# A two-block diffusion transformer forward pass: every third weight slab's low half computed on GpSimd from the context's first projection on

## The chip, the cores and the metric

One core of one Trainium2 chip runs one launch. The metric is the device time of that launch in microseconds (us). Times of single instructions are in us or ns as the profile gives them.

## What is computed

The reference runs two small transformer stacks one after the other on 256 latent tokens and 256 context tokens of width 1024, in float32. The first stack has two layers: adaptive norm, SwiGLU feed-forward (width 2816), a mixer (differential attention beside an mLSTM, then gated linear attention), and a second SwiGLU. The second stack has two layers: multi-head latent attention (MLA) and a 4096-wide squared-ReLU MLP, then neighbourhood attention (NA) and another such MLP, with layer norms after each. Every layer's shifts, scales and gates come from a modulation vector, `silu(c) @ ada_w + ada_b`. The second stack's context stream starts from its own input (`ctx_2`), so its first projections do not depend on the latents that leave the first stack.

```
h = x * (1 + sc1) + sh1;  y, yc = mixer(h, hc)
x = layer_norm(alpha * x + g1 * y)
x = layer_norm(alpha * x + g2 * (relu((x*(1+sc2)+sh2) @ w1)**2 @ w2))
```

## The kernel before, in words

**Split products.** All weights are streamed in 620 slabs of 128x1024 float32 in the order in which they are used (`PLACE` maps a slab's name to its number). Each float32 product is made of three products of TensorE's reduced-precision float32 format (fp32r): ScalarE copies the slab into fp32r (`split_high`, L1614), VectorE subtracts that from the slab to get the low half (`split_low`, L2026), and TensorE computes high x high, high x low and low x high (L2612, L2613, L2614). The activations are split the same way (`h_high`/`h_low`, L2121 and L2113; `hidden_high`/`hidden_low`, L1717 and L2219). A slab feeds 24 matmuls of 256 columns, or half as many of 512.

**One written order.** `order()` yields the steps of the whole pass, and `schedule()` turns each `done` step of a slab s (TensorE has finished with it) into a fetch of slab s+8, `split_high` of s+5 and `split_low` of s+4. Every engine's program walks through this one list and takes the steps that are its own, in order; waits between engines are semaphore counts (`wait_ge`, `mark`). There are 8 raw buffers, 8 low buffers and 6 high buffers: `split_high(s)` waits for the load and for TensorE to have finished slab s-6.

**What each engine does in the order.** ScalarE: `split_high`, activations, squares, high halves. VectorE: `split_low`, the residual additions (L2229), the product after SiLU or ReLU (`mult`/`relu`, L2207 and L2214, one input in PSUM), `hidden_low`, the norms, softmax maxima, and the modulation: for the blocks n = 24 to 239 of the modulation a dot product with the condition vector (`ada`, L2040, shown as CUSTOM_DVE_ANT_0 with two SBUF inputs), one per stream. GpSimd (`pool_program`): the chains of additions for the norms (`add_up`, L1494, one 128x256 addition per feature tile), the scaling of the residual (`plain`, L1557), the rotary products (L1515, L1518), and the loads of the even modulation blocks (`load_ada`, L1472). SyncE issues all other loads, the odd modulation blocks among them. A load of block n waits until VectorE has finished block n-6, since there are six buffers.

**The second stack** interleaves streams: the context's MLA projections and attention run between pieces of the latents' last SwiGLU (`beside_ffn11`), the latents' MLA between pieces of the context's MLP (`beside_mla`), then the latents' MLP with the modulation of the last layer, blocks 204 to 239 (`beside_mlp0`, `ada_pieces`), then NA (`na_steps`) and the last MLP. A layer norm (`layer_norm_groups`) needs two chains of seven GpSimd additions, one for the mean (`add_mean`, then TensorE's `mean_sum`, L2698) and one for the squares (`centre`, then `sum_of_squares`, L2665). For the last two layer norms (`ln10`, `ln11`) VectorE adds the first chain and GpSimd only the squares (`near_centre`); TensorE then reads both sums (`near_sums`, L2684 and L2688).

```
if step[0] == "done" and s + RAWS < N_SLABS:
    yield "fetch", s + RAWS
ahead = HIGHS - 1 if step[0] == "done" else 0
while n_high <= min(s + ahead, N_SLABS - 1):
    yield "split_high", n_high
    n_high += 1
while n_low <= min(s + max(ahead - 1, 0), N_SLABS - 1):
    yield "split_low", n_low
    n_low += 1
```

Of the kernel before, what the change touches and what calls it, by code (L numbers as in the profile page):

```python
# [8 lines left out]
F32 = mybir.dt.float32  # L9
# [20 lines left out]
RAWS, HIGHS = 8, 6  # L30
# [1048 lines left out]
PLACE = places()  # L1079


def schedule():

    n_high = n_low = HIGHS - 1
    for step in order():
        if step[0] not in ("done", "ready"):
            yield step
            continue
        s = PLACE[step[1]]
# [9 lines that stand above are left out]
# [5 lines left out]
class Signal:  # L1104
# [8 lines left out]
    "gla_gate", "ctx2", "na_bv", *(f"rpb{i}" for i in range(4)), "stored",  # L1113
    "gemm", "summed", "swapped", "gates_turned", "scored", "turned", "weighed", "squares_added", "g_spread",
    "spread", "decay_in", "keys_turned", "inner_scored", "state_in", "inner_out", "chunk_in", "chunk_out",
    "split_high", "split_low", "cond_silu", "ada_dot", "ada_block", "mods", "scales", "gates", "squared", "added", "mean", "root", "rstd", "rstd_spread",
    "scaled", "h_high", "h_low", "silu", "relu", "relu_squared", "hidden_raw", "hidden_high", "hidden_low", "x_new",
    "x_final", "x_scaled", "plain", "centred", "near_added", "less_added", "last_added", "ln_scaled", "ln_out", "fm_act", "fm_dve", "tm_act", "tm_dve",
    "gate_act", "gate_dve", "fcol", "floor_act", "lambda_dve", "lambda_act", "rope_sin", "rope_cos", "roped",
# [358 lines left out]
def pool_program(m, pool):  # L1478
# [29 lines left out]
    def near_centre(tag, k, p):  # L1508
        if k < DT - 1:
            square(tag, k, p)  # L1510

    def rope(which, j, bank):
        x, tmp = rope_tile(m, which, j), rope_temp(m, which, j)
        pool.wait_ge("swapped", (which, j))
        do.tensor_tensor(x, x, m.C("cos"), ALU.mult).then_inc(*pool.mark("rope_cos", (which, j)))  # L1515
        pool.wait_ge("rope_sin", (which, j))
        pool.wait_ge("rope_cos", (which, j))
        do.tensor_tensor(x, x, tmp, ALU.add).then_inc(*pool.mark("roped", (which, j)))  # L1518
# [34 lines left out]
    def plain(tag, k, p):  # L1553
        if p not in PLAIN[tag][1]:
# [1 line left out]
        pool.wait_ge("plain", (tag, k, p))  # L1556
        do.tensor_scalar(m.x[:, k, COLS[p]], m.x[:, k, COLS[p]], ALPHA, None, ALU.mult).then_inc(*pool.mark("x_scaled", (tag, k, p)))  # L1557

    work = {"ada": ada, "square": square, "add_mean": add_mean, "centre": centre, "near_centre": near_centre,
            "rope": rope, "da_normalise": da_normalise, "ml_normalise": ml_normalise, "even_norm": even_norm,  # L1560
            "gla_decay3": gla_decay3, "gla_factors": gla_factors, "plain": plain}
    for name, *args in schedule():
# [456 lines left out]
def vector_program(m, dve):  # L2019
    do = dve.do  # L2020
    last_low = [None]

    def split_low(s):
        i = s % RAWS
        dve.wait_ge("split_high", s)
        do.tensor_tensor(m.low[i][:, :], m.raw[i][:, :], m.high[s % HIGHS][:, :].bitcast(F32), ALU.subtract).then_inc(  # L2026
            *dve.mark("split_low", s))
# [571 lines left out]
def tensor_program(m, pe):  # L2599
# [21 lines left out]
    def h_product(bank, tag, s, p):  # L2621

        free(bank)
        pe.wait_ge("split_low", s)
        return products(m.bank[bank][:, 0:T if p == BOTH else NC_TOK], [
            (("h_low", (tag, k, p) if p in H_PARTS.get(tag, (0, 1)) else (tag, k)), *columns_of(s, k), *m.h_term(k, p)) for k in range(DT)])

# [89 lines left out]
    def down(f, c, k, p, bank, at):  # L2717
        n, cols = SIZES[f][c], m.hidden_cols(f, p)
        if at == 0:
            free(bank)  # L2720
        for t in range(at, min(at + 8, n)):
            b = k * n + t
            s, h = PLACE[down_slab(f, c, b)], chunk_at(f, c) + t
            i = h % n_hidden(f)
            pe.wait_ge("split_low", s)
            pe.wait_ge("hidden_low", (f, h))
            last = products(m.bank[bank][:, 0:T if p == BOTH else NC_TOK], [
                (None, *columns_of(s, b % 8), m.hidden[f][i][:, cols], m.hidden_low[f][i][:, cols])],
                start=t == 0, stop=t == n - 1)
            keys = [("x", f, c, k, p), ("down", f, c)] if t == n - 1 else []  # L2730
            if b % 8 == 7:
                keys.append(s)
            if keys:
                last.then_inc(*pe.mark("gemm", *keys))
        read[bank] = "x_new", ("x", f, c, k, p)
# [6 lines left out]
    def out(name, k, half, p, bank):  # L2742
        halves, tag = OUT_HALVES.get(name), H_OF[name]
        keys = [("x", name, k, half, p), *(("out", name, k, half, part) for part in STREAMS_OF[p])]
        if halves:
            s, first = PLACE[SLAB0[name] + 4 * half + k // 2], halves[half]
            free(bank)
            pe.wait_ge("split_low", s)
            terms = [(("h_low", (tag, first + i)), *columns_of(s, k % 2 * 4 + i), *m.h_term(first + i, out_part(name, first + i, p))) for i in range(4)]
            last = products(m.bank[bank][:, 0:T if p == BOTH else NC_TOK], terms)  # L2750
            keys += [s] if k % 2 else []
        else:
            s = PLACE[SLAB0[name] + k]
            last = h_product(bank, tag, s, p)
            keys.append(s)
# [2 lines left out]

    def tm(name, g, half, i, s, banks):
        stage, (_, first, k_slabs, _), s = stage_of(name), TM[name], PLACE[s]  # L2760
        pe.wait_ge("split_low", s)
        for t in range(2):
            tt, bank = 2 * half + t, banks[t]
            if bank is None:
# [257 lines left out]

    def uq(p, i, t, bank):
        s, tag = PLACE[uq_slab(p, i)], of(p, "mla_c")
        pe.wait_ge("split_low", s)
        free(bank)
        products(m.bank[bank][:, 0:NC_TOK], [(("h_low", (tag, k)), *columns_of(s, 2 * k + t), *m.h_term(k, p)) for k in range(4)]
                 ).then_inc(*pe.mark("gemm", ("uq", p, i, t), *([s] if t else [])))
# [1 line left out]

    def uk(p, i, t, bank):
        s, tag = PLACE[SLAB0[of(p, f"mla_uk{i}")]], of(p, "mla_c")
        pe.wait_ge("split_low", s)
        free(bank)
        products(m.bank[bank][:, 0:NC_TOK], [(("h_low", (tag, 4 + k)), *columns_of(s, 4 * k + t), *m.h_term(4 + k, p)) for k in range(2)]
                 ).then_inc(*pe.mark("gemm", ("uk", p, i, t), *([s] if t == 3 else [])))
# [91 lines left out]
```

## Time and profile before

| | |
|---|---|
| median of 3 runs | 2941.49 us (2940.67 to 2943.84) |
| the profiled execution, its own time | 2941.7 us |
| its span, first to last instruction | 2939.9 us |
| busy: PE, VectorE (DVE), ScalarE (ACT), GpSimd (POOL) | 96%, 68%, 43%, 12% |
| mean granted TensorE clock | 0.98 of full |
| slabs whose low half VectorE makes | 620, of which slab 264 is the context's first MLA projection |

PE is TensorE's matmul row and PEld its weight load. A row of a timeline gives the start and the duration in us, the engine and line, the operation, and in brackets the idle time of the engine before it with what ended it. 1704 us is where the low half of slab 264 is computed, so that the stretch from 1704 us to the end at 2940 us is the one in which the change acts.

### The profile page before, as it was taken

The numbers are of one execution on the slowest core, as the hardware profiler recorded it, in microseconds if no ns is written. First come the engines' busy times: TensorE is split into PE (matmuls) and PEld (weight loads), VectorE is DVE, ScalarE is ACT, GpSimd is POOL, SyncE is SP. The second block draws the span as 40 slices with busy tenths as digits, with TensorE's granted clock in tenths as the row PEclk, the third lists the DMA queues.
The fourth block names the chain that finished last, engine by engine and source line by source line (L and its number), as shares of the span: only waits on it lengthen the run. The fifth ranks groups of instructions, "written<-read, shape, count | busy, mean of one in ns | idle before, by whom it ended". The sixth has DMA issues, their size and how long they took to land.

```text
span 2939.9 us, 43428 instructions
## 1 busy us (share of the span) xinstructions
PE 2831.9 (96%) x17424; PEld 2475.1 (84%) x17424; DVE 2010.9 (68%) x3382; ACT 1276.7 (43%) x2094; POOL 340.2 (12%) x380
## 2 busy tenths in 40 slices
PE   7999999988999999999999989999999999999998
PEld 6888897545888889888897889999979999887898
DVE  7789955645687646788655775666656688767764
ACT  4222234443422234222245565556455554645653
POOL 0000010321100001000011110022102210300100
PEclk8999999988999999999999999999999999999999
DMA  6666522101355544555432234455525579553453
GB/s 245 222 224 230 198 86 91 51 29 44 130 206 208 201 143 149 203 202 207 156 106 82 70 132 150 149 180 173 165 78 174 186 279 330 192 155 101 136 187 115
DMA packets 141191, 467.59 MB, mean 159 GB/s; under 512 B 27024, under 2 KB 29200, under 8 KB 140480
## 3 DMA queue, kind: packets, MB, share of 16 engines
q1 hardware_dynamic: 125440, 408.20, 40.9%
q0 software_dynamic: 15552, 56.63, 5.5%
q8 instruction: 138, 2.26, 0.3%
q14 instruction: 61, 0.50, 0.1%
HBM read 463.73 MB, written 1.05 MB: 158 GB/s over the span
## 4 chain that ended last, share of the span: by engine, by line
PE 80%; DVE 11%; ACT 5%; issue 2%; DMA 2%; POOL 1%; SPq 0%; ACTq 0%; DVEq 0%; POOLq 0%
PE bank L2612 24%; PE bank L2614 24%; PE bank L2613 24%; DVE sb_split_low L2026 3%; DVE sb_h_low L2113 1%; PE bank L2902 1%; DMA sb_raw<-weights 1%; PE bank L2883 1%; PE bank L3049 1%; DMA sb_ada_mlp<-ada 1%; PE bank L2843 1%; DVE sb_temp L2040 1%; DVE sb_temp L2107 1%; POOL sb_temp L1494 1%; ACT sb_temp L1931 1%
## 5 line engine op out<-in xcount | busy, mean ns | idle before, releaser
L2612 PE MATMUL bank<-sb_h_high,sb_split_high 128*128 128x256 f32 (+1 forms) x3392 | 1101.8, 325 | 35.2 <-DVE sb_h_low L2121 11.8
L2613 PE MATMUL bank<-sb_h_low,sb_split_high 128*128 128x256 f32 (+1 forms) x3392 | 1085.1, 320 | 0.0
L2614 PE MATMUL bank<-sb_h_high,sb_split_low 128*128 128x256 f32 (+1 forms) x3392 | 1084.6, 320 | 0.0
L1614 ACT ACTIVATE sb_split_high<-sb_raw 128x1024 fp32r<-128x1024 f32 x620 | 646.5, 1051 | 307.8 <-PE bank L2614 288.6
L2026 DVE TENSOR_TENSOR sb_split_low<-sb_raw,sb_split_high 128x1024 fp32r<-128x1024 f32 x620 | 758.7, 1232 | 18.7 <-ACT sb_split_high L1614 18.6
L2612 PEld LDWEIGHTS bank<-sb_h_high,sb_split_high 128*128 128x128 f32 x3392 | 653.1, 193 | 95.2 <-issue 12.5
L2613 PEld LDWEIGHTS bank<-sb_h_low,sb_split_high 128*128 128x128 f32 x3392 | 653.8, 193 | 43.4
L2614 PEld LDWEIGHTS bank<-sb_h_high,sb_split_low 128*128 128x128 f32 x3392 | 653.2, 193 | 43.5
L2040 DVE CUSTOM_DVE_ANT_0 sb_temp<-sb_ada_ffn,sb_cond_ffn 128x1024 bf16<-128x1024 f32 x364 | 429.4, 1218 | 22.8 <-DMA sb_ada_ffn<-ada 22.2
L2612 PE MATMUL bank<-sb_hidden_high_ffn,sb_split_high 128*128 128x512 f32 (+1 forms) x830 | 280.4, 338 | 0.0
L2614 PE MATMUL bank<-sb_hidden_high_ffn,sb_split_low 128*128 128x512 f32 (+1 forms) x830 | 279.2, 336 | 0.0
L2613 PE MATMUL bank<-sb_hidden_low_ffn,sb_split_high 128*128 128x512 f32 (+1 forms) x830 | 279.1, 336 | 0.0
L2229 DVE SCALAR_TENSOR_TENSOR sb_x_res<-bank,sb_gates,sb_x_res 128x256 f32<-128x256 f32 x288 | 132.1, 478 | 172.1 <-PE bank L2614 171.8
L1717 ACT ACTIVATE sb_hidden_high_ffn<-sb_temp 128x512 fp32r<-128x512 f32 (+1 forms) x94 | 52.1, 554 | 339.9 <-DVE sb_temp L2207 339.9
L1704 ACT ACTIVATE sb_temp<-bank 128x256 f32<-128x256 f32 (+1 forms) x158 | 72.8, 461 | 290.3 <-PE bank L2614 290.1
L2207 DVE TENSOR_TENSOR sb_temp<-sb_temp,bank 128x512 f32<-128x512 f32 (+1 forms) x94 | 55.5, 590 | 201.8 <-PE bank L2614 201.3
L2613 PEld LDWEIGHTS bank<-sb_hidden_low_ffn,sb_split_high 128*128 128x128 f32 x830 | 156.3, 188 | 18.6
L2612 PEld LDWEIGHTS bank<-sb_hidden_high_ffn,sb_split_high 128*128 128x128 f32 x830 | 156.2, 188 | 18.6
L2614 PEld LDWEIGHTS bank<-sb_hidden_high_ffn,sb_split_low 128*128 128x128 f32 x830 | 156.2, 188 | 18.5
L2612 PE MATMUL bank<-sb_hidden_high_mlp,sb_split_high 128*128 128x256 f32 x512 | 144.8, 283 | 3.9 <-DVE sb_hidden_low_mlp L2219 3.9
L1472 POOL DMA_DIRECT2D sb_ada_ffn<-ada x90 | 47.8, 532 | 844.6 <-DVE sb_ada_col L2040 844.6
L2614 PE MATMUL bank<-sb_hidden_high_mlp,sb_split_low 128*128 128x256 f32 x512 | 144.0, 281 | 0.0
(329 smaller groups left out, 3487.7 us busy)
## 6 DMA issues: line engine op xcount, KB each, us to landing
sb_raw<-weights SPq DMA_DIRECT2D x620, 512.0 KB, 3.4
sb_ada_ffn<-ada SPq DMA_DIRECT2D x114, 512.0 KB, 4.6
sb_ada_ffn<-ada POOLq DMA_DIRECT2D x90, 512.0 KB, 3.6
sb_ada_mlp<-ada POOLq DMA_DIRECT2D x18, 512.0 KB, 5.5
sb_ada_mlp<-ada SPq DMA_DIRECT2D x18, 512.0 KB, 5.9
sb_cond_ffn<-cond SPq DMA_DIRECT2D x3, 1024.0 KB, 5.4
sb_na_raw<-na_rpb SPq DMA_DIRECT2D x32, 96.0 KB, 6.6
sb_x_res<-tokens SPq DMA_DIRECT2D x4, 512.0 KB, 7.1
```

Of the source, the lines that this page charges most:

```text
L1472: lane.do.dma_start(m.ada[f][i][:, :], m.w["ada"][n, :, :]).then_inc(*lane.mark(ada_signal(n), n, step=16))
L1494: do.tensor_tensor(acc, other if k == 1 else acc, new, ALU.add).then_inc(*pool.mark("added", (kind, tag, k, p)))
L1614: do.activation(m.high[s % HIGHS][:, :], m.raw[s % RAWS][:, :], identity).then_inc(*act.mark("split_high", s))
L1704: do.activation(m.hidden_temp(f, h, p), src, func).then_inc(*act.mark(name, (f, h, p)))
L1717: do.activation(m.hidden[f][i][:, m.hidden_cols(f, p)], m.hidden_temp(f, h, p), identity).then_inc(*act.mark("hidden_high", (f, h, p)))
L2026: do.tensor_tensor(m.low[i][:, :], m.raw[i][:, :], m.high[s % HIGHS][:, :].bitcast(F32), ALU.subtract).then_inc(*dve.mark("split_low", s))
L2040: do.tensor_tensor_reduce(out=m.junk(s), in0=m.ada[f][i][:, :], in1=m.cond[f][:, s, :], scale=1.0, scalar=0.0, op0=ALU.mult, op1=ALU.add, ...
L2207: do.tensor_tensor(temp, temp, src, ALU.mult).then_inc(*dve.mark("hidden_raw", (f, h, p)))
L2229: do.scalar_tensor_tensor(x, m.bank[bank][:, bank_cols(p, s)], m.gates_of(stage)[:, k, s:s + 1], x, ALU.mult, ALU.add).then_inc(*dve.mark( ...
L2612: do.matmul(out, ah, bh, start=start and j == 0, stop=False)
L2613: do.matmul(out, ah, bl, start=False, stop=False)
L2614: last = do.matmul(out, al, bh, start=False, stop=stop and j == len(terms) - 1)
```

## The change

A function names, for a slab, the signal under which its low half is announced: `split_low_pool` for slabs from the context's first projection on (number 264) whose number is divisible by three, `split_low` for all others. VectorE skips the former. `pool_program` gets a `split_low` step that does the same subtraction for them, at the same place of the written order and after the same wait for `split_high`. Each place of `tensor_program` that waits for a slab's low half waits for the named signal.

```diff
+def low_signal(s):
+
+    return "split_low_pool" if s >= PLACE[SLAB0["cmla_down"]] and s % 3 == 0 else "split_low"
...
-    "split_high", "split_low", "cond_silu", "ada_dot", "ada_block", "mods", "scales", "gates", "squared", "added", "mean", "root", "rstd", "rstd_spread",
+    "split_high", "split_low", "split_low_pool", "cond_silu", "ada_dot", "ada_block", "mods", "scales", "gates", "squared", "added", "mean", "root", "rstd", "rstd_spread",
...
+    def split_low(s):
+        if low_signal(s) != "split_low_pool":
+            return
+        i = s % RAWS
+        pool.wait_ge("split_high", s)
+        do.tensor_tensor(m.low[i][:, :], m.raw[i][:, :], m.high[s % HIGHS][:, :].bitcast(F32), ALU.subtract).then_inc(
+            *pool.mark("split_low_pool", s))
...
-    work = {"ada": ada, "square": square, "add_mean": add_mean, "centre": centre, "near_centre": near_centre,
+    work = {"split_low": split_low, "ada": ada, "square": square, "add_mean": add_mean, "centre": centre, "near_centre": near_centre,
...
     def split_low(s):
+        if low_signal(s) != "split_low":
+            return
         i = s % RAWS
         dve.wait_ge("split_high", s)
...
-        pe.wait_ge("split_low", s)
+        pe.wait_ge(low_signal(s), s)
```

The last replacement stands in `h_product`, `down`, `out`, `tm`, `uq` and `uk` alike.

## Rows read from the trace of the kernel before

**Rows 1.** Windows: length, then PE, PEld, DVE, ACT, POOL busy, clock, DMA share, GB/s.

```profile
1704.00:2940.00 1236.00, 1188.97 (x9241) 1128.15 (x9240) 844.55 (x1384) 666.07 (x1141) 156.74 (x158) 0.99 0.52 170
2375.00:2510.00 135.00, 131.13 (x1085) 130.32 (x1084) 123.73 (x197) 61.73 (x93) 7.92 (x15) 0.99 0.85 305
```

**Rows 2.** Waits of the weight loads, 1704 to 2940 us: total, times, longest.

```profile
PEld bank L2612 <- DVE sb_h_low L2121: 10.8, 11, 2.0
...
PEld bank L2612 <- DVE sb_ctx_temp L2214: 5.8, 4, 2.2
...
PEld bank L2612 <- DVE sb_hidden_low_mlp L2219: 4.7, 4, 2.5
...
PEld bank L2612 <- DVE sb_split_low L2026: 3.6, 2, 1.9
```

**Rows 3.** Windows of line L2026 alone (the low halves on VectorE).

```profile
2375.00:2510.00 135.00, 55.77 (x46) 0.99 0.85 305
```

**Rows 4.** Line views of GpSimd's two-input operations: min/median/max ns, first and last start, forms.

```profile
L1494 POOL TENSOR_TENSOR sb_temp<-sb_temp,sb_square x94: 721/740/1774, 393.0 to 2917.3; 128x256 f32<-128x256 f32 x94
L1544 POOL TENSOR_TENSOR sb_odd_big<-sb_odd_big x4: 1263/1266/1288, 1553.9 to 1657.9; 128x512 f32<-128x512 f32 x4
```

**Rows 5.** Timeline: VectorE and GpSimd at 1709 us, then both at 2329 us.

```profile
1710.00 0.96 DVE L2121 TENSOR_TENSOR sb_h_low<-sb_temp,sb_h_high 128x256 fp32r<-128x256 f32 x1
...
1709.48 1.20 POOL L1494 TENSOR_TENSOR sb_temp<-sb_temp,sb_square 128x256 f32<-128x256 f32 x1 [0.22 <-ACT sb_square L1628]
...
2329.36 1.22 DVE L2026 TENSOR_TENSOR sb_split_low<-sb_raw,sb_split_high 128x1024 fp32r<-128x1024 f32 x1
...
2329.52 1.64 POOL L1494 TENSOR_TENSOR sb_temp<-sb_temp,sb_x_res 128x256 f32<-128x256 f32 x1 [1.20 <-DVE sb_x_res L2229]
```

**Rows 6.** Timeline of VectorE in the latents' MLP: one up piece, and the next one's start.

```profile
2399.58 0.41 DVE L2214 TENSOR_TENSOR sb_temp<-sb_temp,bank 128x256 f32<-128x256 f32 x1
2399.91 1.21 DVE L2040 CUSTOM_DVE_ANT_0 sb_temp<-sb_ada_mlp,sb_cond_mlp 128x1024 bf16<-128x1024 f32 x1
...
2401.05 0.41 DVE L2219 TENSOR_TENSOR sb_hidden_low_mlp<-sb_temp,sb_hidden_high_mlp 128x256 fp32r<-128x256 f32 x1
2401.39 1.21 DVE L2026 TENSOR_TENSOR sb_split_low<-sb_raw,sb_split_high 128x1024 fp32r<-128x1024 f32 x1
2402.53 0.41 DVE L2214 TENSOR_TENSOR sb_temp<-sb_temp,bank 128x256 f32<-128x256 f32 x1
```

**Rows 7.** VectorE's longest waits from 2370 to 2510 us, and the loads' times to landing.

```profile
DVE sb_temp L2040 <- DMA sb_ada_mlp<-ada: 7.6, 8, 1.4
DVE sb_hidden_low_mlp L2219 <- ACT sb_hidden_high_mlp L1717: 1.9, 4, 0.5
...
DMA to landing us min/median/max: 4.1/5.8/7.3
```

**Rows 8.** Timeline: loads of blocks 226 (GpSimd) and 227 (SyncE), their dots, and ScalarE's slab 486.

```profile
2440.64 0.53 POOL L1472 DMA_DIRECT2D sb_ada_mlp<-ada  x1 [7.53 <-DVE sb_ada_col L2040]
...
2456.51 0.43 SPq L1472 DMA_DIRECT2D sb_ada_mlp<-ada  x1
...
2460.41 1.22 DVE L2040 CUSTOM_DVE_ANT_0 sb_temp<-sb_ada_mlp,sb_cond_mlp 128x1024 bf16<-128x1024 f32 x1
...
2463.42 1.21 DVE L2040 CUSTOM_DVE_ANT_0 sb_temp<-sb_ada_mlp,sb_cond_mlp 128x1024 bf16<-128x1024 f32 x1
...
2452.57 1.04 ACT L1614 ACTIVATE sb_split_high<-sb_raw 128x1024 fp32r<-128x1024 f32 x1
```

**Rows 9.** Timeline at two layer norms: GpSimd's last additions and the matmul that needs them.

```profile
1913.63 1.64 POOL L1494 TENSOR_TENSOR sb_temp<-sb_temp,sb_x_res 128x256 f32<-128x256 f32 x1 [0.35 <-DVE sb_x_res L2229]
...
1915.74 0.59 PE L2698 MATMUL bank<-sb_temp,sb_const 128*128 128x256 f32 x2
...
2723.98 5.47 POOL L1494 TENSOR_TENSOR sb_temp<-sb_temp,sb_square 128x256 f32<-128x256 f32 x5 [0.59 <-ACT sb_square L1628]
...
2729.79 0.61 PE L2684 MATMUL bank<-sb_const,sb_rstd 128*128 128x1 f32 x4 [1.63 <-DVE sb_rstd L2157]
```

More of the change, by code:

```diff
@@ L2724, in down @@
             i = h % n_hidden(f)
-            pe.wait_ge("split_low", s)
+            pe.wait_ge(low_signal(s), s)
             pe.wait_ge("hidden_low", (f, h))
@@ L2747, in out @@
             free(bank)
-            pe.wait_ge("split_low", s)
+            pe.wait_ge(low_signal(s), s)
             terms = [(("h_low", (tag, first + i)), *columns_of(s, k % 2 * 4 + i), *m.h_term(first + i, out_part(name, first + i, p))) for i in range(4)]
@@ L2760, in tm @@
         stage, (_, first, k_slabs, _), s = stage_of(name), TM[name], PLACE[s]
-        pe.wait_ge("split_low", s)
+        pe.wait_ge(low_signal(s), s)
         for t in range(2):
@@ L3024, in uq @@
         s, tag = PLACE[uq_slab(p, i)], of(p, "mla_c")
-        pe.wait_ge("split_low", s)
+        pe.wait_ge(low_signal(s), s)
         free(bank)
@@ L3032, in uk @@
         s, tag = PLACE[SLAB0[of(p, f"mla_uk{i}")]], of(p, "mla_c")
-        pe.wait_ge("split_low", s)
+        pe.wait_ge(low_signal(s), s)
         free(bank)
```

## The prediction, made before the changed kernel ran

> **What bounds the kernel now.** I read the windows first, then the waits, then the timelines of the places they point to. In the stretch where the change acts the weight loads fill 1128 of 1236 us at a clock of 0.99, and VectorE 845 us [rows 1]. TensorE sets the time, then, and VectorE can give back only what TensorE waits for it. That is little: the four largest such waits are 10.8, 5.8, 4.7 and 3.6 us, 25 us in all [rows 2]. Only 3.6 us name the low half itself. The reader is to see that 119 subtractions leave VectorE (slabs 264 to 618, every third), at 1.14 us of queue each (from 2401.39 to 2402.53) [rows 6] 136 us of its work, and that a gain has at most 25 us, and most likely a third of that, to come from.
>
> One window is different. From 2375 to 2510 us, the latents' MLP with the last modulation blocks, VectorE is busy 123.7 of 135 us [rows 1], and its idle time is waiting for modulation loads (7.6 us) and for ScalarE (1.9 us) [rows 7], hardly for TensorE. In an up piece its instructions stand back to back: product, dot, hidden low half, slab low half, 2.95 us from one product to the next (2399.58 to 2402.53) [rows 6]. TensorE needs less: 135 us less the 4.7 it waits [rows 1, 2], over 1085 matmuls, is 0.12 us a matmul, and 24 of them, a slab, are 2.88 us. There VectorE is as much the bound as TensorE, and those 4.7 us are TensorE waiting for hidden low halves [rows 2].
>
> **The price of the moved instruction.** No row shows a 128x1024 operation on GpSimd. Alone, 256 columns take 740 ns (the median) and 512 take 1263 [rows 4]. The line through both gives 740 + 3 x 523 = 2.31 us. The ends are VectorE's 1.22 us [rows 5], were the format or size to favour it, and 4 x 0.74 = 2.96 us. I take 2.31, because both sizes lie on one line with a small fixed part.
>
> **What it does to VectorE.** The timelines show the two engines stopping each other. A VectorE subtraction of 256 columns takes 0.96 us at 1710.00, behind GpSimd's addition, where the usual one takes 0.43; and GpSimd's addition of 0.74 us takes 1.64 when it begins 0.16 us into a VectorE subtraction of 1.22 [rows 4, 5]. In the latter case 1.22 - 0.16 = 1.06 us of waiting plus 0.74 is 1.80, so GpSimd stood still nearly all the time and then ran. I take it that one waits for the other, full length, when both read two SBUF tensors. Products with an input in PSUM go on. The Trainium skill (SBUF — State Buffer, section "SBUF: two separate sides") calls the shared port pair "an exclusive lock, not a bandwidth split", held for the whole instruction; it speaks against this change, and the rows agree within their 0.2 us. Under that rule the sum is the one below, and under plain sharing it would be the faster rival's.
>
> **Term A, 2375 to 2510 us.** 46 low halves fall in it [rows 3], so 15 move. Each frees 1.14 us of VectorE. Its operation on GpSimd, 2.31 us, starts when VectorE's running subtraction ends; the product beneath it goes on (0.33 us, from 2399.58 to 2399.91), then the dot waits for the rest, 1.98 us [rows 6]. Net 1.98 - 1.14 = +0.84 us, times 15 = +12.6 us of VectorE. Of that its 7.6 us of waiting for loads are absorbed [rows 7], since SyncE issues the odd blocks at TensorE's pace and a later VectorE finds them landed: +5.0.
>
> The even blocks' loads sit in GpSimd's queue and are moved too, past its new waits. Today GpSimd runs ahead: block 226 is issued at 2440.6 for a dot at 2460.4, while SyncE's block 227 is issued at 2456.5 for a dot at 2463.4 [rows 8]. Behind the subtraction of slab 486, whose high half ScalarE ends at 2453.6, block 226 cannot go before 2453.6 + 2.3 = 2455.9; with the median 5.8 us to landing it is there at 2461.7, 1.3 us late, and with 7.3 us 2.8 late [rows 7, 8]. Going through all 18 even blocks in this way, with each one's own time to landing, I find three or four late by 1 to 3 us and the rest early by 0.5 to 10: +3. Nothing is lost if VectorE lags anyway; if GpSimd's operation itself waits 1.1 us each time, some eight are late and it is +8. **Sum of A: +8** (0 to +20).
>
> **Term B, the norms' chains.** GpSimd now puts a 2.3 us subtraction inside chains of additions that TensorE waits for. In the context's first layer norm the last addition ends at 1915.27 and the matmul that needs it starts at 1915.74 [rows 9]: under 0.5 us to spare, and slab 321's subtraction stands between two of the additions. The chain idles some 0.35 us ahead of each pair and saves a wait or two for VectorE, so +1.2. The latents' first norm has the same pattern (slab 414): +1.4. The square chain of the latents' second norm (slab 513) has about 1.3 us to spare: +1.3. In the NA norm the chain of five additions ends at 2729.45, 0.34 us ahead of the first matmul of the sums [rows 9], slab 558's subtraction stands in it, and no other work covers it: +2.0. In the others the additions come 2.88 us apart or the subtraction falls outside. **Sum of B: +6** (0 to +14).
>
> **Term C, the attention stretches.** VectorE works there in short chains (maximum, reciprocal, scaling, which may wait behind GpSimd) with a subtraction of its own less per moved slab. One against the other: +1 (-2 to +5).
>
> **Term D, what VectorE gives back.** Outside A and B its waits of 10.8, 5.8 and 3.6 us are 17 events [rows 2]; a third of them, about 5 or 6, have a moved subtraction ahead, worth at most 1.14 us each: 6.5, less what is blocked elsewhere: **-5** (-10 to 0).
>
> At no cost, because others cover them: the later low halves themselves. They are made four slabs ahead, 4 x 2.88 = 11.5 us of TensorE, against at most 2.3 + 1.2 us on GpSimd. The 104 moved subtractions outside A fall mostly where VectorE has a third of its time free; if that cover went, each would cost A's 0.84 us.
>
> **Sum.** +8 + 6 + 1 - 5 = +10 us. The profiled execution's own time is 2941.7, so 2951.7 us; it lies 0.2 us above the median, which gives **2951.5 us**.
>
> **The rivals.**
>
> *No change.* TensorE is the bound and the written order has slabs and banks enough: blocks of 2 us on VectorE vanish in its free third. For it: nowhere outside A does VectorE reach 90% for long, and the additions may regroup. Against it: A has no free time at all. It would give A +3, B +3, C 0, D -5: 2942.
>
> *Faster.* The end on the other side: VectorE's queue in A. If GpSimd's subtraction blocked VectorE by less than the 1.14 us it frees, A's step would fall from 2.95 us on average by 0.2, under TensorE's 2.88, and the 4.7 us of waiting for hidden halves would go; the same freedom gives D its full 6.5. 2941.5 - 11 = 2930. It decides at a block of 1.14 us per moved slab. Against it: the 0.96 us subtraction at 1710 [rows 5].
>
> *The loads decide.* GpSimd's loop in A, high half, subtraction (2.3, or 3.5 when it waits), load (5.8), dot, becomes the pace, so that eight even blocks come late and each lateness reaches TensorE: A +16, the rest as forecast: 2960. For it: SyncE's loads already land just as VectorE asks [rows 7]. Against it: GpSimd's queue passes a moved slab only every third slab.
>
> That the change does nothing of what it says I exclude: the test on the slab's number is the same for maker, skipper and reader.
>
> **How the numbers follow.** Forecast 0.44, no change 0.27, faster 0.15, the loads 0.14. A measurement of this kernel tells about 0.2% (5.9 us) from none, so the bounds are 2935.6 and 2947.4. The forecast's own range, from its terms, is 2944 to 2962; I count its lower edge with the slower side. Hence faster 0.15, same 0.28, slower 0.57. The range reaches down into the no-change case and nearly to the faster one, 2936, and up past the loads, 2966.
>
> **What would show it.** The new subtractions on GpSimd: 119 at 2.3 us alone, up to 3.5 when VectorE runs; VectorE's own busy time in the last 1236 us down by less than 145, with dots and subtractions of over 2 us among them (a blocked instruction shows as a long one). In A: the waits of TensorE for hidden low halves up from 4.7 to about 12 us, GpSimd's waits for the dots (block n-6) gone and even loads landing within some 3 us of their dots. In the NA norm: the first matmul of the sums 2 us later against the last product before it. I am wrong if dots and low halves on VectorE keep their 1.22 us, if the waits in A do not grow, or if the norm chains end as early as now.

## The result, and the profile after

The changed kernel takes 2967.49 us (median of 4 runs, 2963.61 to 2971.95), the kernel before 2942.17 us beside it: ratio 1.0084, 95% interval 1.0071 to 1.0098, which is 24.7 us more (0.84% of 2942.17; 20.9 to 28.8). The prediction said 2951.5, between 2936 and 2966. The direction is right, the size is not, and the time lies above the range. The profiled execution took 2966.69 us (span 2964.6).

In the new files the lines have moved by up to 15: the subtraction is L2041 on VectorE and the new one L1522 on GpSimd, the dot L2055, the low halves L2136 and L2234, the first product L2627. First the page of the changed kernel, busy times and the two groups of low halves, then GpSimd's group by line (minimum, median and longest, in ns):

```profile
PE 2841.2 (96%) x17424; PEld 2480.6 (84%) x17424; DVE 1982.2 (67%) x3263; ACT 1276.7 (43%) x2094; POOL 643.9 (22%) x499
...
L2041 DVE TENSOR_TENSOR sb_split_low<-sb_raw,sb_split_high 128x1024 fp32r<-128x1024 f32 x501 | 651.1, 1305 | 22.1 <-ACT sb_split_high L1627 22.1
L1522 POOL TENSOR_TENSOR sb_split_low<-sb_raw,sb_split_high 128x1024 fp32r<-128x1024 f32 x119 | 319.2, 2683 | 645.8 <-ACT sb_split_high L1627 641.7
```

```profile
L1522 POOL TENSOR_TENSOR sb_split_low<-sb_raw,sb_split_high x119: 2339/2682/3489, 1704.3 to 2932.2; 128x1024 fp32r<-128x1024 f32 x119
```

GpSimd got its 119 subtractions: 2.34 us when nothing holds them up, 2.68 in the median, 3.49 at worst. VectorE lost 119 instructions, which should have taken 136 us off its 2010.9 us; it lost 29. The rest came back inside its other instructions, whose work has not changed: a slab's low half, for one, took 1232 ns in the mean before and takes 1305 now. The timelines below show them standing still.

The windows, and VectorE's and the weight loads' waits, of the latents' MLP (2375 to 2510 us before, the same work now from 2382 to 2533):

```profile
core 0: us, PE busy (x) PEld busy (x) DVE busy (x) ACT busy (x) POOL busy (x), PEclk, DMA share, GB/s
2382.00:2533.00 151.00, 135.93 (x1089) 134.06 (x1088) 133.59 (x182) 62.51 (x93) 53.55 (x34) 0.97 0.80 284
```

```profile
engine line waited for: us in total, times, longest us
DVE sb_temp L2055 <- DMA sb_ada_mlp<-ada: 12.1, 7, 2.8
...
PEld bank L2627 <- DVE sb_hidden_low_mlp L2234: 9.1, 5, 3.5
PEld bank L2627 <- issue: 7.8, 5, 4.1
```

Against [rows 1, 2, 7]: the stretch is 151 us in place of 135. VectorE is busy 133.6 in place of 123.7 although 15 or 16 instructions of 1.22 us have gone; its waits for modulation loads are 12.1 us in place of 7.6; TensorE's waits for hidden low halves 9.1 in place of 4.7.

The timelines of GpSimd, VectorE and TensorE in 2466 to 2485 us show both at work:

```profile
2468.23 2.82 POOL L1522 TENSOR_TENSOR sb_split_low<-sb_raw,sb_split_high 128x1024 fp32r<-128x1024 f32 x1 [7.79 <-ACT sb_split_high L1627]
2471.00 0.58 POOL L1477 DMA_DIRECT2D sb_ada_mlp<-ada  x1
2477.25 2.40 POOL L1522 TENSOR_TENSOR sb_split_low<-sb_raw,sb_split_high 128x1024 fp32r<-128x1024 f32 x1 [5.67 <-ACT sb_split_high L1627]
2479.61 0.57 POOL L1477 DMA_DIRECT2D sb_ada_mlp<-ada  x1
2480.20 2.74 POOL L1522 TENSOR_TENSOR sb_split_low<-sb_raw,sb_split_high 128x1024 fp32r<-128x1024 f32 x1
```

```profile
2468.70 0.41 DVE L2229 TENSOR_TENSOR sb_temp<-sb_temp,bank 128x256 f32<-128x256 f32 x1
2469.03 3.10 DVE L2055 CUSTOM_DVE_ANT_0 sb_temp<-sb_ada_mlp,sb_cond_mlp 128x1024 bf16<-128x1024 f32 x1
...
2478.61 2.13 DVE L2055 CUSTOM_DVE_ANT_0 sb_temp<-sb_ada_mlp,sb_cond_mlp 128x1024 bf16<-128x1024 f32 x1 [2.85 <-DMA sb_ada_mlp<-ada]
2480.67 0.08 DVE L2055 DVE_READ_ACCUMULATOR2_ANT sb_ada_col<- 128x1 f32 x1
2480.67 2.56 DVE L2234 TENSOR_TENSOR sb_hidden_low_mlp<-sb_temp,sb_hidden_high_mlp 128x256 fp32r<-128x256 f32 x1
```

```profile
2484.51 0.36 PE L2627 MATMUL bank<-sb_hidden_high_mlp,sb_split_high 128*128 128x256 f32 x1 [3.90 <-DVE sb_split_low L2041]
```

GpSimd's subtraction runs from 2468.23 to 2471.05. The product, with one input in PSUM, begins 0.47 us into it and takes its usual 0.41. The dot, with two inputs in SBUF, takes 3.10 in place of 1.22: it ends 1.08 us after the subtraction, its own length, less the overlap that the records have. Then comes the second effect. GpSimd issues block 226's load (2471.00) only behind that subtraction; in the kernel before this load went out 19.8 us ahead of its dot [rows 8]. VectorE now idles 2.85 us for it. Third, the next subtraction, which starts at 2480.20 while a dot is still running, holds up the hidden low half behind that dot: 2.56 us in place of 0.41. Behind it in VectorE's queue stands the low half of a slab (2483.15, 1.21 us), and for that the matmul at 2484.51 had waited 3.90 us.

TensorE's clock comes on top of the waits. The matmuls at 2484.70 and 2484.82 are 0.12 us apart; soon after that wait of 3.90 us they come every 0.21 us, because the granted clock has fallen to 0.50, the lower of its two levels (1.2 GHz in place of 2.4):

```profile
2485.50:2488.00 2.50, 2.50 (x14) 2.50 (x14) 2.47 (x7) 0.00 (x0) 0.00 (x0) 0.50 0.71 280
```

Over the whole stretch the mean granted clock is 0.97, and 0.99 before. By estimate that costs up to 151 x 0.03 - 135 x 0.01 = 3.2 us of what the stretch loses; up to, because TensorE isn't busy all the time. The prediction had no term for it.

Where the 25 us lie. The table compares the start of the same weight load in two traces, by stretches of the kernel before (us). A trace has some 2 us of its own variation: ahead of 1700 us the kernels do not differ, and in 2375-2510 e2 and e6 show +2.1 each and move nothing there.

| kernel | to 1700 | 1700-1800 | 1800-1960 | 1960-2120 | 2120-2375 | 2375-2510 | 2510-2710 | to the end | sum |
|---|---|---|---|---|---|---|---|---|---|
| changed | -1.2 | +3.2 | +3.0 | +2.3 | -0.1 | +15.6 | -1.7 | +3.4 | +24.7 |
| e1, MLP only | +0.1 | +0.4 | 0.0 | 0.0 | -1.1 | +19.5 | -1.2 | -0.7 | +17.0 |
| e2, all but MLP | +1.0 | +3.3 | +3.1 | +2.2 | -0.3 | +2.1 | -2.0 | +2.1 | +11.4 |
| e3, waits only | +2.8 | 0.0 | 0.0 | 0.0 | -0.2 | +1.4 | +0.6 | +0.2 | +4.9 |
| e4, even loads early | +3.4 | +3.3 | +3.0 | +4.5 | -0.3 | +10.4 | -2.2 | +2.1 | +24.3 |
| e11, all loads early | -2.3 | +3.3 | +3.1 | +4.5 | -0.2 | +4.6 | -2.3 | +2.8 | +13.4 |
| e5, first five | +3.4 | +4.3 | 0.0 | 0.0 | -0.4 | -1.6 | -2.0 | +0.1 | +3.9 |
| e6, spared places | +3.0 | -0.2 | 0.0 | +2.3 | +0.5 | +2.1 | -1.9 | -0.3 | +5.5 |
| e7, no read | +0.8 | -4.4 | -1.0 | -1.5 | -4.7 | -3.9 | -2.8 | -0.9 | -18.4 |
| e9, no read, 8 pieces | +0.8 | -4.4 | -1.0 | -1.5 | -4.6 | -2.6 | -4.4 | -0.8 | -18.4 |
| e12, no read, 32 pieces | +2.7 | -2.4 | -1.0 | -1.5 | -4.1 | -2.8 | -5.3 | -0.2 | -14.6 |
| e8, odd loads early | +0.6 | +0.4 | +0.1 | 0.0 | -1.1 | -5.6 | 0.0 | +0.1 | -5.4 |
| e10, e8 and five moves | +2.4 | -2.7 | +0.1 | -1.5 | -2.1 | -5.6 | -1.6 | -0.7 | -11.5 |

### The profile page after: what moved, and what is told of

It reads as the page before. It is cut to its first block, busy times and chain, and to the rows that moved or that the text cites. A ratio compares the mean times of both kernels' runs of the same rounds, so it can differ in the third digit from the quotient of the medians.

```text
span 2964.6 us, 43436 instructions
## 1 busy us (share of the span) xinstructions
PE 2841.2 (96%) x17424; PEld 2480.6 (84%) x17424; DVE 1982.2 (67%) x3263; ACT 1276.7 (43%) x2094; POOL 643.9 (22%) x499
## 4 chain that ended last, share of the span: by engine, by line
PE 77%; DVE 11%; ACT 5%; issue 2%; DMA 2%; POOL 1%; SPq 0%; ACTq 0%; POOLq 0%; DVEq 0%
PE bank L2627 23%; PE bank L2629 23%; PE bank L2628 23%; DVE sb_split_low L2041 3%; DMA sb_ada_mlp<-ada 1%; ACT sb_split_high L1627 1%; DVE sb_h_low L2128 1%; PE bank L2917 1%; DVE sb_temp L2055 1%; DMA sb_raw<-weights 1%; POOL sb_temp L1499 1%; PE bank L2898 1%; DVE sb_h_low L2136 1%; PE bank L3064 1%; PE bank L2858 1%
## 5 line engine op out<-in xcount | busy, mean ns | idle before, releaser
L2627 PE MATMUL bank<-sb_h_high,sb_split_high 128*128 128x256 f32 (+1 forms) x3392 | 1102.5, 325 | 40.9 <-DVE sb_h_low L2136 17.4
L2627 PEld LDWEIGHTS bank<-sb_h_high,sb_split_high 128*128 128x128 f32 x3392 | 653.0, 192 | 102.4 <-DVE sb_h_low L2136 18.1
L2041 DVE TENSOR_TENSOR sb_split_low<-sb_raw,sb_split_high 128x1024 fp32r<-128x1024 f32 x501 | 651.1, 1305 | 22.1 <-ACT sb_split_high L1627 22.1
L1522 POOL TENSOR_TENSOR sb_split_low<-sb_raw,sb_split_high 128x1024 fp32r<-128x1024 f32 x119 | 319.2, 2683 | 645.8 <-ACT sb_split_high L1627 641.7
L2055 DVE CUSTOM_DVE_ANT_0 sb_temp<-sb_ada_ffn,sb_cond_ffn 128x1024 bf16<-128x1024 f32 x364 | 429.6, 1220 | 23.1 <-DMA sb_ada_ffn<-ada 14.4
L2627 PE MATMUL bank<-sb_hidden_high_ffn,sb_split_high 128*128 128x512 f32 (+1 forms) x830 | 280.7, 338 | 2.0 <-DVE sb_x_res L2244 2.0
L2627 PEld LDWEIGHTS bank<-sb_hidden_high_ffn,sb_split_high 128*128 128x128 f32 x830 | 156.3, 188 | 21.3 <-DVE sb_x_res L2244 2.8
L2629 PEld LDWEIGHTS bank<-sb_hidden_high_ffn,sb_split_low 128*128 128x128 f32 x830 | 156.3, 188 | 18.4
L2627 PE MATMUL bank<-sb_hidden_high_mlp,sb_split_high 128*128 128x256 f32 x512 | 146.4, 286 | 12.0 <-DVE sb_hidden_low_mlp L2234 8.0
```

The lines of the kernel that those rows point to most:

```text
L2055: do.tensor_tensor_reduce(out=m.junk(s), in0=m.ada[f][i][:, :], in1=m.cond[f][:, s, :], scale=1.0, scalar=0.0, op0=ALU.mult, op1=ALU.add, ...
L2627: do.matmul(out, ah, bh, start=start and j == 0, stop=False)
L2629: last = do.matmul(out, al, bh, start=False, stop=stop and j == len(terms) - 1)
```

## The experiments

The theory after the result: GpSimd's subtraction shuts VectorE's two-input work out for its whole length, which costs where TensorE already hangs on VectorE, and lets the modulation loads slip. The rivals: the longer and more often waiting queue of GpSimd does it without any blocking; or every moved slab costs its share. In the results, "less" and "more" are the ratio times the 2944 us of the kernel before; in brackets stands the 95% interval.

### e1 and e2: the change by place

```diff
-    return "split_low_pool" if s >= PLACE[SLAB0["cmla_down"]] and s % 3 == 0 else "split_low"
+    return "split_low_pool" if 459 <= s <= 504 and s % 3 == 0 else "split_low"
```

e2 moves the others, from 264 on, and leaves 459 to 504.

> Only the slabs 459 to 504 divisible by three go to GpSimd (16 of the 119), those of the latents' MLP in which VectorE has no free time; all others stay on VectorE. Theory (that stretch costs +15.6 us of the 24.7 us between the two traces, because VectorE is the bound there): +13 to +17 us over the kernel before. Rival (the cost is spread evenly, 0.21 us per moved slab): +3 us. Second rival (the lag of 7 us that the changed kernel brings into the stretch is what tips it): +5 to +10 us.

> The other 103 slabs go to GpSimd, 459 to 504 stay on VectorE. Theory: +7 to +10 us over the kernel before. Even spread: +22 us. If the stretches outside were harmless (no change in themselves): 0.

e1: 2958.85 us, ratio 1.0048 (1.0031 to 1.0065), 14.1 us more, as expected. e2: 2954.53 us, ratio 1.0035 (1.0022 to 1.0048), 10.3 us more, just over the 7 to 10 expected. Together 24.4 of the 24.7 us: the two parts add up, and 16 of the 119 moved slabs, those of the latents' MLP, carry more than half. That e1's stretch shows +19.5 us in its trace, more than the changed kernel's +15.6, is in part the clock: its mean is 0.94 there. e2 also shows that the rest is no +2 us, as terms B, C and D had it together, but 10.

### e3: the wait without the subtraction

The kernel before; GpSimd waits for the high halves of the 16 slabs 459 to 504 at the places where the changed kernel subtracts, and does nothing.

```diff
+    def split_low(s):
+        if 459 <= s <= 504 and s % 3 == 0:
+            pool.wait_ge("split_high", s)
...
+    work = {"split_low": split_low, "ada": ada, "square": square, "add_mean": add_mean, "centre": centre, "near_centre": near_centre,
```

> The kernel before, but GpSimd waits for ScalarE's high half at the places of the 16 slabs 459 to 504 and does no subtraction there; VectorE makes all low halves. It shows the loads' new place in GpSimd's queue by itself. If the queue matters: even loads land 2 to 10 us ahead of their dots in place of 12 to 18, some late, +2 to +5 us. If only the two engines' blocking of each other matters: 0 within 1 us.

2945.24 us, ratio 1.0005 (0.9996 to 1.0014), 1.5 us more (-1.2 to +4.1), between the two expectations (0 within 1, and 2 to 5). VectorE's waits for loads go from 7.6 to 9.1 us:

```profile
DVE sb_temp L2044 <- DMA sb_ada_mlp<-ada: 9.1, 8, 2.2
```

The even blocks, which had landed 12 us or more ahead of their dots, now land 0 to 11 us ahead. The wait uses up the slack of the queue and hardly more.

### e4 and e11: the changed kernel with earlier loads

```diff
-        if n % 2 == 0 and n >= 24:
+        if n % 2 == 0 and 24 <= n < 204:
             load_ada(m, pool, n)
+        if n == 204:
+            load_ada(m, pool, n)
+        if n % 2 == 0 and 204 <= n < 238:
+            load_ada(m, pool, n + 2)
```

e11 has this and the same for the odd blocks in SyncE's program (see e8).

> The changed kernel, but GpSimd issues the load of the even block n+2 at the place of block n in the last modulation's stretch, so that its loads no longer wait behind the subtractions next to them. If late loads carry a good part of the stretch: VectorE's waits for even blocks go and the time falls by 3 to 7 us against the changed kernel, to 2960 to 2964. If blocking alone does it: 2967 within 1.5 us.

> The changed kernel with both kinds of modulation loads of the latents' MLP issued one block of their kind earlier, the even ones by GpSimd and the odd ones by SyncE. If lateness of loads is what the prediction's term A missed, VectorE's 12 us of waiting for them go to under 3, and the loss in that stretch falls from 15.6 us to what is left of blocking: VectorE's 123.7 us of work, plus some 28 us of blocks, less 16 x 1.22 us, against 135 us, 0 to +3 us: 2951 to 2956 us in all. If blocking alone decides, it stays at the 2964 us of the early even loads.

e4: 2964.13 us, ratio 1.0068 (1.0053 to 1.0083); e11: 2956.91 us, ratio 1.0050 (1.0036 to 1.0064). The loss falls from 24.7 to 20.0 and to 14.7 us, and in the stretch itself from 15.6 to 10.4 and 4.6 us. e4's gain of 4.7 us in time (3 to 7 had been expected) is within the intervals; its stretch and e11 carry the reading. e11's waits and window in the MLP:

```profile
DVE sb_temp L2063 <- DMA sb_ada_mlp<-ada: 3.9, 2, 2.6
...
PEld bank L2635 <- DVE sb_hidden_low_mlp L2242: 5.2, 2, 3.4
```

```profile
2383.00:2523.00 140.00, 133.22 (x1089) 132.28 (x1088) 129.99 (x181) 63.31 (x94) 55.60 (x34) 0.98 0.86 307
```

The load waits are 3.9 us, not quite the under 3 expected, and the time is 1 us over the 2951 to 2956 expected. Early loads take 10 of the 24.7 us away. But not all of these ten are the change's doing: e8, below, takes 6.5 us off the kernel before by the same means, for the odd loads alone. With early loads on both sides the change still costs 14.7 + 6.5 = 21.2 us, and in the stretch 4.6 + 5.6 = 10.2 of the 15.6. What it adds in lateness is 5.4 us by the traces, and 3.5 us in time, which is less than the intervals can tell. The order of the programs says how it comes about: the subtraction, lengthened by what blocks it, sits in front of the even loads, and the odd loads leave when SyncE has passed the slab fetches, which follow TensorE, which follows VectorE. The bare wait in the queue (e3) loses 1.5 us.

### e5 and e6: where a move costs

e5 moves slabs 264 to 276 alone; e6 moves 79 slabs and spares those places:

```diff
-    return "split_low_pool" if s >= PLACE[SLAB0["cmla_down"]] and s % 3 == 0 else "split_low"
+    return "split_low_pool" if (279 <= s <= 318 or 342 <= s <= 408 or 423 <= s <= 456 or 525 <= s <= 552 or 561 <= s) and s % 3 == 0 else "split_low"
```

> Only slabs 264 to 276 are moved (five subtractions, 1704 to 1745 us). In the changed kernel this stretch cost 3.8 us, beside 16 us blocked nowhere else near it, and the prediction had given it nothing. If the cause is there (GpSimd's subtraction holds back VectorE's low halves of the activations, for which TensorE waits at 1713 and 1720 us), the stretch shows +3 to +4 us again and the run takes 3 to 4 us more than the kernel before. If the 3.8 us were an effect of something earlier or of chance, the two kernels agree within 1 us in that stretch.

> 79 of the 119 subtractions are moved: all but those where the changed kernel's trace shows VectorE without slack (264 to 276, 321 to 339, 411 to 420, 459 to 522, 555 to 558). If a block costs only where TensorE already hangs on VectorE, two thirds of the moves cost nothing together: 2942 to 2948 us. If every block costs its 0.8 us, as in the latents' MLP, it is 79 x 0.84 = 66 us more; if each moved slab costs the same share of the 24.7 us, 79/119 of it, 2960 us. VectorE should still show 79 x 1.2 us less of its own work, and nearly as much in instructions made longer.

e5: 2948.72 us, ratio 1.0015 (1.0006 to 1.0023), 4.4 us more (1.8 to 6.8) for five moves, as good as the 3 to 4 expected. In its trace +2.8 us have come up by 1760 us, where the changed kernel has +3.8; the rest of its +4.3 comes at 1764 us of the kernel before, where TensorE's clock falls behind a wait of 1.7 us that the kernel before has as well. e6: 2945.57 us, ratio 1.0006 (0.9998 to 1.0015), 1.8 us more (-0.6 to +4.4) for 79 moves. Not a share per slab, then, but the place. What happens at the first five is in the changed kernel's timeline:

```profile
1718.72 2.34 POOL L1522 TENSOR_TENSOR sb_split_low<-sb_raw,sb_split_high 128x1024 fp32r<-128x1024 f32 x1
```

```profile
1719.34 2.87 DVE L2136 TENSOR_TENSOR sb_h_low<-sb_temp,sb_h_high 128x256 fp32r<-128x256 f32 x2 [0.91 <-ACT sb_h_high L1698]
```

```profile
1721.39 0.29 PEld L2627 LDWEIGHTS bank<-sb_h_high,sb_split_high 128*128 128x128 f32 x1 [2.59 <-DVE sb_h_low L2136]
```

In the kernel before the same two low halves took 1.27 us for both (at 1718.68). Here they take 2.87, and TensorE, which takes them tile by tile, waits 2.59 us. In e6 the blocking is there as well (GpSimd's 79 subtractions have a mean of 2685 ns, as all 119 had):

```profile
L1522 POOL TENSOR_TENSOR sb_split_low<-sb_raw,sb_split_high 128x1024 fp32r<-128x1024 f32 x79 | 212.0, 2685 | 524.6 <-ACT sb_split_high L1627 520.6 <-DVE sb_x_res L2244 4.0
```

VectorE, at 1974.1 us, is down by 37 us where 79 x 1.14 = 90 were freed, so 53 us of it are blocked time (I had expected nearly all). That costs next to nothing in time, so it falls on instructions that nobody waits for.

### e7, e9 and e12: the same queue, without a read

The changed kernel with one line of GpSimd's step replaced; in these three the low half of every third slab is zeros. e9 writes them in 8 pieces of 128 columns, e12 in 32 of 32.

```diff
-        do.tensor_tensor(m.low[i][:, :], m.raw[i][:, :], m.high[s % HIGHS][:, :].bitcast(F32), ALU.subtract).then_inc(
+        do.memset(m.low[i][:, :].bitcast(F32), 0.0).then_inc(
```

> As the changed kernel, with the same waits at the same places, but GpSimd fills the low half with zeros in place of the subtraction: it writes the same 128x1024 elements and reads nothing (the low half of every third slab is left out of the computation). If GpSimd's reading is what blocks VectorE, VectorE's instructions keep their usual durations, the 119 x 1.14 us are really free, and the time falls below the kernel before, to 2930 to 2938 us. If the length of the steps in GpSimd's queue (the additions of the norms and the even loads behind a waiting step) is what costs, 5 us or more of the 24.7 stay: over 2947 us.

> As the run with zeros in place of the subtraction, but the zeros are written in eight pieces of 128 columns, so that GpSimd is held longer for each low half (one piece of 1024 took 0.95 us; eight should take 1.5 to 3 us, near the subtraction's 2.34). The low half of every third slab is again left out of the computation. If only GpSimd's reading costs, the time stays near the 2925 us of the short fill (2922 to 2932). If the length of the step in GpSimd's queue was a real part of the changed kernel's loss, 5 us or more come back: over 2932 us.

> Again zeros in place of the subtraction, now in 32 pieces of 32 columns. Eight pieces had lengthened the step only from 0.95 to 1.22 us, which does not reach the subtraction's 2.34. By the 0.04 us that each further piece cost there, 32 pieces take some 2.2 us, so GpSimd's queue is now held as long as by the subtraction, still without a read. The low half of every third slab is again left out. If only the reading costs, the time stays at 2922 to 2932 us. If the length of the step was a part of the loss, 5 us or more come back, over 2932 us, and it shows where the additions of the norms are late.

e7: 2924.65 us, ratio 0.9937 (0.9922 to 0.9952), 18.5 us less than the kernel before. e9: 2923.98 us, ratio 0.9940 (0.9927 to 0.9954). e12: 2928.53 us, ratio 0.9951 (0.9935 to 0.9968), 14.4 us less. e7 is below the 2930 to 2938 expected, e9 and e12 are inside theirs. GpSimd's step in the three, from the groups of e7 and the timelines of e9 and e12:

```profile
L1522 POOL MEMSET sb_split_low<- 128x1024 f32 x119 | 113.5, 954 | 771.1 <-ACT sb_split_high L1627 764.9 <-DVE sb_x_res L2244 5.9
```

```profile
2474.55 1.07 POOL L1523 MEMSET sb_split_low<- 128x128 f32 x7 [10.32 <-ACT sb_split_high L1629]
2475.57 0.20 POOL L1524 MEMSET sb_split_low<- 128x128 f32 x1
```

```profile
1708.17 1.91 POOL L1523 MEMSET sb_split_low<- 128x32 f32 x31
1710.03 0.11 POOL L1524 MEMSET sb_split_low<- 128x32 f32 x1
```

The step takes 0.95, 1.22 and 1.97 us. e9's was too short to say much (1.5 to 3 had been expected); e12's is near the subtraction's 2.34 (though not its median of 2.68) and costs 3 us more than e9's, with overlapping intervals: in the traces 3.8, of which 1.9 lie ahead of 1700 us and 2.0 in 1700-1800, beside the first norm. So the length of the step may be worth some 2 us, not 24.7. In all three GpSimd has the changed kernel's waits at the changed kernel's places. The subtraction and its reads are gone, and the time drops by 39 to 43 us against the changed kernel. That TensorE multiplies zeros is not what does it: its commonest matmul (L2627) takes 324 ns in the mean in e7 and 325 in the changed kernel. VectorE in e7, on its page and in its window of the MLP:

```profile
PE 2827.1 (97%) x17424; PEld 2470.5 (85%) x17424; DVE 1877.8 (64%) x3263; ACT 1276.6 (44%) x2094; POOL 437.2 (15%) x499
```

```profile
2364.00:2495.00 131.00, 129.36 (x1084) 128.78 (x1083) 106.88 (x181) 61.31 (x92) 22.74 (x33) 1.00 0.91 326
```

VectorE is busy 133 us less than before in place of 29: the full price of the moved work. The Trainium skill ("SBUF — State Buffer", section "SBUF: two separate sides") says that a VectorE operation with two SBUF inputs contends "only against a GpSimd op that reads SBUF"; e7 agrees, with 1877.8 us of VectorE against 1982.2.

### e8 and e10: a faster kernel

e8 is the kernel before, with only SyncE's odd blocks from 207 on issued one odd block earlier; e10 adds GpSimd's subtraction for five slabs, ahead of which TensorE had waited for VectorE.

```diff
-        if n % 2 or n < 24:
+        if n < 24 or n % 2 and n < 205:
             load_ada(m, sp, n)
+        if n == 205:
+            load_ada(m, sp, n)
+        if n % 2 and 205 <= n < 239:
+            load_ada(m, sp, n + 2)
...
+    return "split_low_pool" if s in (279, 378, 417, 423, 552) and s % 3 == 0 else "split_low"
```

> The kernel before, with the odd modulation loads from block 207 on issued by SyncE one odd block earlier (block n+2 at the place of block n). Nothing is moved to GpSimd. In the kernel before, VectorE waits 7.6 us for modulation loads in the latents' MLP and TensorE 4.7 us for hidden low halves there. If VectorE's own work is the bound of that stretch, as the prediction had it, both waits go and the run takes 3 to 5 us less than the kernel before (2937 to 2941). If VectorE only waits there because it is ahead of TensorE anyway, the waits move to other causes and the time stays within 1 us.

> The early odd loads (2937 us) and only five moved subtractions: slabs 279, 378, 417, 423 and 552, ahead of which TensorE waited for VectorE and waited 1 to 1.7 us less in the changed kernel or in the one with spared places. If such a move is worth there what the trace of those kernels shows, and costs nothing elsewhere, 4 to 6 us less than with the early loads alone: 2931 to 2934 us. If the gains there are passed on to the next wait, 2936 to 2938 us.

e8: 2936.98 us, ratio 0.9978 (0.9969 to 0.9987), 6.5 us less. e10: 2930.23 us, ratio 0.9962 (0.9948 to 0.9976), 11.2 us less, faster than both kernels and a little better than the 2931 to 2934 expected. Its interval (7.1 to 15.3 less) overlaps e8's (3.8 to 9.1); in the traces its further 6 us lie at the moved places, -3.1 in 1700-1800 and -1.5 in 1960-2120 among them. e8's waits in the MLP (the first two rows VectorE's, the last TensorE's) and its window:

```profile
DVE sb_x_res L2233 <- PE bank L2618: 3.1, 4, 1.2
...
DVE sb_temp L2044 <- DMA sb_ada_mlp<-ada: 0.4, 1, 0.4
...
PEld bank L2616 <- DVE sb_hidden_low_mlp L2223: 0.8, 2, 0.5
```

```profile
2375.00:2505.00 130.00, 129.57 (x1090) 129.16 (x1089) 123.86 (x198) 63.78 (x94) 7.92 (x15) 1.00 0.88 317
```

The same VectorE work, 123.9 us, now fits into 130 us, TensorE is busy for 129.6 of them, and VectorE waits for TensorE. The load waits of the kernel before were on the path: not slack of VectorE's, but 5.6 us of TensorE's time: 3.9 us of waits for hidden low halves (4.7 against 0.8) and, by estimate, 1.4 us of clock (135 x 0.01; it is 1.00 here).

## Why the prediction was right or wrong

**The price** of the operation on GpSimd was right: 2.31 us forecast, 2.34 alone. That the two engines shut each other out for the whole length was right too, and e7 shows that it is the subtraction with its reads that does it, not the write. So was the sign, and the place that matters most.

**Term A** (forecast +8, measured +15.6 in the trace; e1 gives +14.1) has two halves. VectorE's own work, block less relief, was +12.6; the windows say 133.6 - 123.7 = +9.9. What failed is the next step, "of that its 7.6 us of waiting for loads are absorbed", and the +3 for the even loads behind it, -4.6 in sum. VectorE's idle time did not shrink from 11.3 us (135 - 123.7) but grew to 17.4 (151 - 133.6), +6.1. The waits for loads, one by one (the dots run in the order of the blocks), show both steps failing. In the kernel before, all eight are for odd blocks, 7.6 us. In the changed kernel three are for odd blocks, 4.4 us, and four for even ones, 7.7 us. Two of them, for the even block 220 and the odd block 233:

```profile
2452.44 1.23 DVE L2055 CUSTOM_DVE_ANT_0 sb_temp<-sb_ada_mlp,sb_cond_mlp 128x1024 bf16<-128x1024 f32 x1 [2.23 <-DMA sb_ada_mlp<-ada]
2506.98 2.35 DVE L2055 CUSTOM_DVE_ANT_0 sb_temp<-sb_ada_mlp,sb_cond_mlp 128x1024 bf16<-128x1024 f32 x1 [2.61 <-DMA sb_ada_mlp<-ada]
```

So 3.2 us were absorbed in place of 7.6, and the even blocks cost 7.7 us in place of 3. The prediction had counted the late even blocks rightly, "three or four late by 1 to 3 us" (they are 2.4, 2.2, 2.8 and 0.2 us late), and then let VectorE's lag swallow most of it. For the odd blocks it had two loops as if they were independent: "SyncE issues the odd blocks at TensorE's pace and a later VectorE finds them landed". But when VectorE is the bound, TensorE is late by just as much, and so are SyncE's fetches and the odd loads behind them. e8 shows that this loop cost 5.6 us already before the change, and e11 that with loads issued early the stretch takes 140 us against e8's 130: +10, of which VectorE's busy time is 130.0 - 123.9 = 6.1. The clock's share, up to some 3 us, is a term that the prediction did not have.

The rival in which the loads decide had the size (A +16) but not the mechanism alone: it had the waiting GpSimd queue as the pace, which e3 prices at 1.5 us (-1.2 to +4.1). Behind a real subtraction the even loads cost more than behind that wait: GpSimd and VectorE take turns, and the subtraction stands in front of the load.

**Terms B, C and D** came to +2 in sum; e2 gives +10.3. B's places were partly right, for partly other reasons. The NA norm: forecast +2.0; +2.2 of the +3.4 in the changed kernel's last stretch stand at it. But the first matmul of the sums came only 0.55 us later than before against the last product (a wait of 2.18 us in place of 1.63), not the 2 us named as a sign. And that wait is for VectorE's own chain, whose addition L2172 was shut out by the moved subtraction and took 2.12 us in place of 0.50; for GpSimd's chain the next sums waited 0.93 us more. The rest is the clock, at 0.50 from 2751.5 to 2758 us. GpSimd's rows, then TensorE's and VectorE's:

```profile
2744.95 2.74 POOL L1499 TENSOR_TENSOR sb_temp<-sb_temp,sb_square 128x256 f32<-128x256 f32 x3 [0.59 <-ACT sb_square L1641]
2747.64 3.33 POOL L1522 TENSOR_TENSOR sb_split_low<-sb_raw,sb_split_high 128x1024 fp32r<-128x1024 f32 x1
2750.93 1.77 POOL L1499 TENSOR_TENSOR sb_temp<-sb_temp,sb_square 128x256 f32<-128x256 f32 x2
```

```profile
2751.31 0.97 PE L2699 MATMUL bank<-sb_const,sb_rstd 128*128 128x1 f32 x4 [2.18 <-DVE sb_rstd L2172]
2753.22 1.01 PE L2703 MATMUL bank<-sb_const,sb_temp 128*128 128x1 f32 x4 [0.93 <-DVE sb_temp L2176]
...
2749.14 2.12 DVE L2172 TENSOR_TENSOR sb_rstd<-sb_rstd,sb_x_res 128x256 f32<-128x256 f32 x1
2752.74 0.43 DVE L2176 TENSOR_TENSOR sb_temp<-sb_temp,sb_square 128x256 f32<-128x256 f32 x1 [1.48 <-POOL sb_temp L1499]
```

The context's first norm: forecast +1.2. TensorE is no later behind it (0.0 us at 1924 us of the kernel before). The stretch's +3.0 comes further on, at 1948 to 1956 us, where two of VectorE's own slab low halves are shut out, one after the other, and TensorE waits 2.0 us for the residual additions that stand behind them:

```profile
1957.09 3.30 DVE L2041 TENSOR_TENSOR sb_split_low<-sb_raw,sb_split_high 128x1024 fp32r<-128x1024 f32 x1
...
1961.10 2.87 DVE L2041 TENSOR_TENSOR sb_split_low<-sb_raw,sb_split_high 128x1024 fp32r<-128x1024 f32 x1
```

The latents' norms: forecast +2.7, nothing measured (-0.1 and -1.7 in their stretches).

What B did not have at all is the place at 1700 to 1745 us (+3.2 by then in the changed kernel's trace; e5 shows it alone, 4.4 us in time). The prediction had read its own warning there, the 0.96 us low half at 1710.00 [rows 5], as evidence of the lock and not as a place where TensorE takes VectorE's low halves as they come, 10.8 us of waits [rows 2]. It costed GpSimd's delayed additions in the norm chains and not VectorE's blocked two-input links next to them. C, +1, was +2.3.

**Term D** (-5) was there, and larger than thought where nothing is blocked: TensorE no longer waits 1.7 us at 1763.8 us for slab 279 and 1.5 us at 2087 us for slab 379, whose low half stood behind the moved one of slab 378 in VectorE's queue; e10 takes five such places for 4.7 us less than e8 (0.9962 against 0.9978, with overlapping intervals). Of "a gain has at most 25 us, and most likely a third of that" the bound held and the third was too low: without the read the gain is 14 to 18 us. In the changed kernel the blocks eat it.

The no-change rival's argument, that blocks of 2 us vanish in VectorE's free third, is true at 79 of the 119 places (e6, +1.8 us) and false at the other 40, which cost the rest. Left open is how the 4 us are divided that neither e1, e5 nor e6 has (24.7 - 14.1 - 4.4 - 1.8 = 4.4, with an interval of several us on each): the 19 remaining slabs, most of them around norms, were not run alone.

## What to carry to other kernels

Before moving two-input elementwise work from VectorE to GpSimd, price it as VectorE's time, not as free time: GpSimd's duration (here 2.34 us) less what VectorE saved (1.14), wherever VectorE's next instruction reads two SBUF tensors. Then look at each place for who takes VectorE's results as they come; an average of free time says nothing. And do not let a wait be "absorbed" by a slower engine before asking who triggers what is waited for: if the trigger follows the slowed engine, the wait stays. Here issuing 17 loads one step earlier gave 6.5 us, and moving 119 instructions lost 24.7.

## What the runs showed of the hardware

A fill of 128x1024 float32 on GpSimd, which reads nothing, takes 0.95 us and leaves VectorE's subtractions and dots at their 1.22 us; a subtraction of the same size on GpSimd takes 2.34 us alone and stretches a dot to 3.10 and a 256-column low half from 0.41 to 2.56 us. The custom dot with two SBUF inputs is shut out like a plain subtraction, the product with an input in PSUM is not (0.41 us at 2468.70, in the middle of GpSimd's subtraction). In e9 and e12 cutting the fill into more pieces cost about 0.03 to 0.04 us a piece: (1.22 - 0.95) / 7 and (1.97 - 0.95) / 31. TensorE's granted clock was 0.50 for a while behind its waits of 3.90 us (2484.51) and 2.18 us (2751.31) in the changed kernel, and 1.00 throughout the latents' MLP in e7 and e8, where its waits for hidden low halves add up to 2.0 and 0.8 us.
